# New due times for the steps woven into the expert rows, and the second half's weights held back until the last rows have landed

## The chip, the cores and the metric

The kernel runs on 1 core of one Trainium2 chip. The metric is the device time of one launch in microseconds (us), lower is better. A core has a matrix engine (PE, TensorE), a vector engine (DVE), a scalar engine (ACT), GpSimd (POOL) and a sync engine (SP) that here only issues transfers; each works through its own list of instructions in order and waits on semaphores. Transfers issued by SP and POOL run on the core's 16 DMA engines.

## The reference, cut to what matters

512 tokens of 1024 channels go through two blocks, all in 32-bit floats.

- First block: a convolution mixer, then a layer of experts. For each token 8 heads pick 16 of 16384 experts each, so 128 experts a token:

```python
u_sel = jnp.take(u, idx, axis=0)
act = jax.nn.gelu(jnp.einsum("chkd,cd->chk", u_sel, xc))
v_sel = jnp.take(v, idx, axis=0)
return jnp.einsum("chk,chkd->cd", act * gates, v_sel)
```

- Second block: a feed-forward layer (`x + 0.5 * (silu(x @ w_gate) * (x @ w_up)) @ w_down`, hidden width 2816), two causal attentions of 8 heads each (one with a forget gate, one with latent projections) whose outputs are gated, added and projected, and a second feed-forward layer of the same kind.

## The kernel before, in words

**Expert rows.** Tokens are held as 4 tiles of 128 (one token a partition). An expert "row" is one of the 512 pairs (tile, rank): for row `i`, POOL issues an indirect DMA (L2424) that gathers for each of the 128 tokens of tile `i // 128` its expert's `u` and `v` (128 x 2048 floats, 1 MB) into one of 7 buffers `pair`. DVE then forms the dot product (`dot`, L1728), ACT turns it into a weight with five tiny activations (`weigh`), and the weighted `v` is added to `resid`: for rows before 264 mostly by PE (a diagonal matmul), from row 264 on by DVE (`add_row`, L1062, 128 x 1024), two rows behind the dot. POOL may gather row `i` only when row `i - 7` was added.

**Two halves.** The second block is computed in two halves of 256 tokens. Half A (tiles 0 and 1, which are ready after 256 rows) runs while rows 264 to 511 are still being gathered; half B (tiles 2 and 3) runs after the last row. In half A, PE multiplies the weights as they come; in half B each weight chunk is first split into a rounded part and a rest (`rounded` on ACT, `split` on DVE), and three matmuls stand for one.

**Order of the woven steps.** PE runs half A's matmuls as fast as their inputs allow (it has no expert rows by then). On DVE, ACT and POOL, half A's steps are a generator that yields a due time before each step (`when(stage, n)`), and the class `Paced` releases, after expert row `i`, all steps that are due by `clock(i)`. So the place of each step among the rows is fixed when the program is built, by two things: the plan's clock (`Plan.add`, `Plan.ring` and the numbers in `plan_banks`, which add so many us for each use of a PSUM bank) and the table `PACE`, which says how many us each of the next so many rows is worth:

```python
def until(self, us):
    while self.due is not None and self.due <= us:
        self.due = next(self.steps, None)
```

I write "after row 499" for a step that stands after the dot of row 499 and the `add_row` of row 497. A step that is placed too early makes its engine wait, with all later rows behind it; one that is placed too late only makes PE's result sit in its bank.

**Stages of half A**: `norm1A`, `up1A` (22 chunks of gate and up weights, the products multiplied on DVE into `hidden`), `down1A` (4 banks: output half h, tile i; both tiles of one output half are finished almost together, since `rows_times` goes through the chunks with the two tiles inside), `norm_mA`, projections (`latA`, `fqA`, `fkA`, `fvA`), attention (38 steps n: the scores of head n are reduced on DVE at L1470 and exponentiated on ACT, transposed on PE three steps later, copied by ACT, multiplied with the values at step n + 4; after every 8 heads DVE scales the result into `ym`, L1056; PE also computes the gates of the output in between, `GATE_AT`), branches (`brA`), `woA`, and then the feed-forward stages `norm2A`, `up2A`, `down2A`.

**Weights.** SP issues the loads of all weight chunks (up to 1 MB each) in the order `ORDER` into three buffers `raw` (`loads`, `chunk`, L548); a load waits until the chunk three before it was used. For half A "used" is a PE semaphore; for half B it is the second part's split on DVE. The half's results are stored by SP as well (`store`, L566), where `ORDER` reaches chunk 3 of half B's first feed-forward layer.

Of the kernel before, what the change touches and what calls it, by code (L numbers as in the profile page):

```python
# [84 lines left out]
W = {}  # L85
# [6 lines left out]
NPAIR = 7  # L92
PAIRS = 512
# [1 line left out]
START_ROW = 264  # L95


PACE = ((64, 3.85), (25, 3.3), (28, 2.1), (36, 2.85), (22, 2.6), (64, 3.85), (PAIRS, 2.6))


def clock(row):

    at, left = 0.0, row - START_ROW
    if left < 0:
        return 2.6 * left
    for n, us in PACE:
        if left <= n:
# [27 lines left out]
class Plan:  # L135
# [4 lines left out]

    def add(self, stage, banks, us=0.0, told=True):

        n = sum(1 for k in self.uses if k[0] == stage)
        for j, b in enumerate(banks):
            self.fills[b] += told
            self.outs[b] += 1
            self.clock += us
            self.uses[stage, n + j] = Use(b, self.outs[b] - 1, self.fills[b], self.outs[b], self.clock)

    def ring(self, stage, n, us=0.0):  # L150
# [18 lines left out]
def plan_banks():  # L169
    p = Plan()  # L170
    for stage, n in (("norm0", 10), ("cf", 16), ("sc", 16), ("bg", 4)):
        p.ring(stage, n)
    p.add("y_sc", [0, 1, 4, 5])
    p.add("ms_sc", [6])
    p.add("y_sc", [2, 3, 7, 0])
    p.add("mean", [1])
    p.add("var", [1])
    p.add("ms_cf", [6, 7])
    p.add("y_cf", [4, 5, 2, 3, 6, 7, 4, 5])
    p.add("hn", [0, 1])  # L180
    for c, (h, a, b) in enumerate(CALLS):
        p.add("q", [0, 1])
        p.add("S", [2, 3])
        if c == 0:
            p.add("hn", [0, 1, 2, 3, 0, 1])
    for t in range(3):
        p.add("mix", [6, 7] if t == 1 else [4, 5], told=False)
    p.clock = 0.0
    for x in "AB":
        p.at = 6  # L190

        def ffn(f):
            p.clock += 8.0
            p.ring(f"norm{f}{x}", 4, 1.5)
            if x == "A":
                p.ring(f"up{f}{x}", 22, 7.0)
            else:
                for stage, n in (("up", 1), ("rate", 1), ("up", 21)):
                    p.ring(f"{stage}{f}{x}", n, 7.0)
            p.ring(f"down{f}{x}", 4, 19.0)  # L200

        ffn(1)
        p.clock += 8.0
        for stage, n, us in (("norm_m", 4, 1.5), ("lat", 2, 5.0), ("fq", 2, 7.0), ("ratem", x == "B", 0.0), ("fk", 2, 7.0),
                             ("cum", 1, 3.0), ("fv", 2, 7.0), ("tfq", 4, 1.0), ("tfk", 4, 2.0), ("tlat", 2, 1.0)):
            p.ring(stage + x, n, us)
        p.add("gate" + x, [4] if x == "A" else [5, 5], 6.0)
        p.add("look" + x, [0, 1] * 8, 3.3)
        p.add("look" + x, [0, 1] * 8, 6.2)
        p.add("turn" + x, [2, 3] * 16)  # L210
        p.add("prep" + x, [6, 7] * 8)
        for blk in range(4):
            p.add("o" + x, [4 + blk % 2], told=False)
            p.add("fin" + x, [4 + blk % 2], 2.0)
            if blk in (1, 2):
                p.add("gate" + x, [3 + blk])
        p.add("gate" + x, [6, 7, 6, 7, 6] if x == "A" else [6, 7, 6, 7])
        p.at = 0
        for stage, n, us in (("br", 16, 1.8), ("wo", 4, 7.0)):
            p.ring(stage + x, n, us)  # L220
        ffn(2)
    return p

# [63 lines left out]
def program(nc, x, meta, wts, uv, rows, cols, pos, ident, tri, mask, out):  # L287
    with ExitStack() as ctx:
# [3 lines left out]
        def sem(name):  # L292
            return ctx.enter_context(nc.semaphore(name))

        B = plan_banks().uses
# [58 lines left out]
        pairs_in = [sem(f"pair_landed{i}") for i in range(NPAIR)]  # L354
# [145 lines left out]
        def through(e, key):  # L500

            end = ENDS[key]
            if isinstance(end, int):
                e.wait_ge(w_used, end)
            else:
                e.wait_ge(full[B[end].bank], B[end].nth)
# [7 lines left out]
        def taken(e, stage, n):  # L514

            b = B[stage, n]
            e.wait_ge(outs[b.bank], b.after)
# [17 lines left out]
        def when(stage, n):  # L535
            return B[stage, n].when


        def loads(e):
            def chunk(c):  # L540
                if c.i >= 3:
                    was = W[ORDER[c.i - 3][0]]
                    if was.s is not None:
                        e.wait_ge(w_lo, 2 * was.s + 2)
                    else:
                        through(e, was.key)
                at_ = CHUNKS[c.key[0]][0] + c.key[1]
                e.dma_start(wbufs[c.slot][:, 0:c.n], wts[at_, :, 0:c.n]).then_inc(w_in[c.slot], 16)  # L548

            e.dma_start(h0[0:16, :], meta).then_inc(meta_in, 16)  # L550
            e.dma_start(resid[:, 0, :], x[0:P, :]).then_inc(x_in[0], 16)
            e.dma_start(idt[:], ident[0]).then_inc(const_in, 16)
            e.dma_start(colt[:], cols).then_inc(const_in, 16)
            for t in range(1, NT):
                e.dma_start(resid[:, t, :], x[t * P:(t + 1) * P, :]).then_inc(x_in[t], 16)
            for key, _ in ORDER[0:3]:
                chunk(W[key])
            for dst, src in ((onest, ident[1]), (ones1, ident[2]), (trit, tri), (maskf, mask), (rowt, rows),
                             (postt, pos)):
                e.dma_start(dst[:], src).then_inc(late_in, 16)  # L560
            def store(p):
                for h in range(2):
                    for i in range(2):
                        t = T0[p] + i
                        taken(e, "down2" + p, 2 * h + i)
                        e.dma_start(out[t * P:(t + 1) * P, h * 512:(h + 1) * 512],  # L566
                                    resid[:, t, h * 512:(h + 1) * 512]).then_inc(stored, 16)

            for key, _ in ORDER[3:]:
                if key == ("f1", 3, "B"):  # L570
                    store("A")
                chunk(W[key])
                if key == ("wout", 3):
                    filled(e, "bg", 3)
                    e.dma_start(kbuf, wts[CHUNKS["keys"][0]]).then_inc(keys_in, 16)
            store("B")
            e.wait_ge(stored, 16 * 2 * NT)
# [470 lines left out]
        def vector(e):  # L1048
# [414 lines left out]
            def attention(p):  # L1463
                t0, nth = T0[p], NTH[p]
                for n in range(38):
                    yield when("look" + p, min(n, 31))
                    if n < 32:
                        t, h, a = t0 + n % 16 // 8, n % 8, n // 8 % 2
                        o, _ = filled(e, "look" + p, n)
# [1 line left out]
                    if p == "B" and 3 <= n < 35:  # L1471
                        r = n - 3
# [13 lines left out]
                    if p == "B" and n >= 6 and (n - 6) % 8 == 7:  # L1486
                        r = (n - 6) // 8
# [4 lines left out]
                    if 4 <= n < 36 and (n - 4) % 8 == 7:  # L1492
                        r = n - 4
                        blk, a = r // 8, r // 8 % 2
# [314 lines left out]
        def scalar(e):  # L1809
# [257 lines left out]
            def attention(p):  # L2067
                t0, nth = T0[p], NTH[p]
                for n in range(38):
                    yield when("look" + p, min(n, 31))  # L2070
                    if n < 32:
                        h, a = n % 8, n // 8 % 2
                        w = (t0 + n % 16 // 8 + 1) * P
# [8 lines left out]
                    if p == "A" and 3 <= n < 35:  # L2082
                        r = n - 3
# [15 lines left out]
                    if n >= 6 and (n - 6) % 8 == 7:  # L2099
                        blk = (n - 6) // 8  # L2100
# [211 lines left out]
            for n in range(32):  # L2312
                steps = scores_in_steps(n + 2) if n < 8 else iter(())
                for k in range(16):
                    i, j = 16 * n + k, (16 * n + k) % 8
# [249 lines left out]
```

## Time and profile before

| | |
|---|---|
| median of 3 runs | 2482.41 us (2480.25 to 2482.93) |
| the profiled execution's own time | 2480.95 us |
| its span (first to last instruction) | 2479.1 us, 28622 instructions |
| mean granted TensorE clock | 0.932 |
| busy over the span | PE 85%, DVE 74%, ACT 48%, POOL 31% |
| moved by DMA | 760.89 MB: 536.90 MB by POOL's gathers, 222.15 MB by SP |

How to read it: the span falls into the first block's convolution (to about 250 us), the rows before 264 (to about 930 us), half A beside rows 264 to 511 (to about 1859 us) and half B (the rest). Busy shares are averages over these and don't tell what bounds any of them; for that the chain that ended last, the waits and the windows of one stage have to be read. In the timeline a group's row gives its start, its duration, and in brackets how long the engine sat idle before it and what released it. In a table of windows the columns are the busy time of PE, PE's weight load, DVE, ACT and POOL, then the granted clock, the DMA engines' busy share and GB/s.

### The profile page before, as it was taken

Reading aid. Unit: us, or ns where it says so; the run is one execution under the profiler, and the core shown is the slowest. Engines: PE = TensorE matmul, PEld = TensorE weight load, DVE = VectorE, ACT = ScalarE, POOL = GpSimd, SP = SyncE. Lnnn points to the kernel's source line nnn. Section 1 sums busy time; section 2 is a strip of 40 time slices with the busy share of each in tenths; the row PEclk is TensorE's granted clock in tenths of the full one; section 3 lists DMA queues with packets and bytes.
Section 4 is the critical chain, followed back from the end, with each engine's and each line's share of the span. In section 5 each row is a group of like instructions: output and inputs, shape, how many; then the busy total and the mean of one; then the engine's idle time right before and its main releaser. Section 6 shows DMA issues by size and latency. Waiting matters only on the chain.

```text
span 2479.1 us, 28622 instructions
## 1 busy us (share of the span) xinstructions
PE 2111.2 (85%) x9508; PEld 1500.0 (61%) x9508; DVE 1833.3 (74%) x3372; ACT 1180.2 (48%) x3776; POOL 760.6 (31%) x634
## 2 busy tenths in 40 slices
PE   6987898988877777999684578699949999999999
PEld 6965443443222225884343466488529988798997
DVE  6985676868888888887898987776576656567564
ACT  5214556555666664442455554433234436344443
POOL 0001444454555553232465643433220001100000
PEclk9988999999999998999795699899979999999999
DMA  5211999999999998999999999999984544124553
GB/s 210 72 68 58 382 415 421 417 413 421 421 421 420 415 417 346 387 419 398 379 417 353 363 414 365 396 397 421 386 355 170 187 167 167 69 86 155 186 187 136
DMA packets 107460, 760.89 MB, mean 307 GB/s; under 512 B 12064, under 2 KB 12832, under 8 KB 16432
## 3 DMA queue, kind: packets, MB, share of 16 engines
q0 software_dynamic: 73728, 536.90, 53.2%
q1 hardware_dynamic: 33584, 222.15, 23.7%
q8 instruction: 76, 1.25, 0.2%
q14 instruction: 72, 0.59, 0.1%
HBM read 756.91 MB, written 2.10 MB: 306 GB/s over the span
## 4 chain that ended last, share of the span: by engine, by line
PE 44%; DVE 9%; DMA 4%; issue 3%; ACT 1%; POOL 1%; DVEq 0%; ACTq 0%; POOLq 0%
PE bank L582 43%; DVE resid L1062 4%; DMA pair<-in_uv,idx 4%; DVE pair L1728 2%; PE bank L1019 0%; DVE half L1056 0%; DVE tmp L1056 0%; POOL smalls L2373 0%; PE bank L892 0%; POOL pair L2424 0%; DVE smalls L1384 0%; PE bank L825 0%; ACT half L1813 0%; DVE smalls L1470 0%; ACT frow L1813 0%
## 5 line engine op out<-in xcount | busy, mean ns | idle before, releaser
L2424 POOL DMA_INDIRECT pair<-in_uv,idx x512 | 649.6, 1269 | 874.8 <-DVE resid L1062 556.5
L1813 ACT ACTIVATE smalls<-smalls 128x1 f32<-128x1 f32 x2058 | 540.5, 286 | 665.1 <-DVE smalls L1728 647.0
L1728 DVE CUSTOM_DVE_ANT_0 pair<-pair,hn 128x1024 f32<-128x1024 f32 x512 | 624.1, 1220 | 155.4 <-DMA pair<-in_uv,idx 153.8
L582 PE MATMUL bank<-pair,diag 128*128 128x512 f32 x928 | 460.8, 629 | 118.2 <-ACT diag L1813 117.3
L582 PEld LDWEIGHTS bank<-pair,diag 128*128 128x128 f32 x928 | 169.3, 195 | 390.9 <-ACT diag L1813 245.9
L582 PE MATMUL bank<-ft,raw 128*128 128x256 f32 x1664 | 371.8, 387 | 12.0 <-DVE ft L1056 12.0
L1062 DVE SCALAR_TENSOR_TENSOR resid<-pair,smalls,resid 128x1024 f32<-128x1024 f32 x280 | 358.7, 1281 | 0.9 <-DVE resid L1062 0.5
L582 PEld LDWEIGHTS bank<-ft,raw 128*128 128x128 f32 x1664 | 323.1, 195 | 56.6 <-issue 12.5
L1056 DVE TENSOR_TENSOR half<-raw,half 128x1024 fp32r<-128x1024 f32 (+1 forms) x204 | 235.6, 1194 | 124.4 <-ACT half L1813 124.3
L1813 ACT ACTIVATE half<-raw 128x1024 fp32r<-128x1024 f32 (+1 forms) x204 | 199.4, 1025 | 129.0 <-PE bank L582 128.9
L582 PE MATMUL bank<-ft_hi,half 128*128 128x256 f32 x960 | 178.0, 286 | 2.6 <-DVE ft_early L1056 1.5
L582 PEld LDWEIGHTS bank<-ft_hi,half 128*128 128x128 f32 x960 | 150.9, 191 | 3.2 <-issue 1.8
L582 PE MATMUL bank<-raw,hidden 128*128 128x512 f32 x352 | 151.4, 593 | 0.0
L1813 ACT ACTIVATE smalls<-smalls,gat 128x1 f32<-128x1 f32 x512 | 143.2, 280 | 0.0
L582 PE MATMUL bank<-ft_late_hi,half 128*128 128x256 f32 x704 | 126.1, 282 | 2.3 <-DVE ft_late_lo L1056 2.3
L582 PE MATMUL bank<-ht,raw 128*128 128x512 f32 (+2 forms) x320 | 123.3, 529 | 0.7 <-ACT ht L1813 0.7
L2348 POOL TENSOR_TENSOR smalls<-smalls,mh 128x1 f32<-128x1 f32 (+1 forms) x21 | 15.8, 759 | 342.3 <-DVE smalls L1059 341.9
L582 PEld LDWEIGHTS bank<-raw,hidden 128*128 128x128 f32 x352 | 67.1, 191 | 83.1 <-issue 83.0
L582 PE MATMUL bank<-half,hidden_hi 128*128 128x512 f32 x352 | 110.9, 396 | 1.6 <-DVE half L1056 1.6
L582 PEld LDWEIGHTS bank<-ft_late_hi,half 128*128 128x128 f32 x704 | 108.4, 189 | 2.6 <-issue 2.5
L1813 ACT ACTIVATE diag<-idt,smalls 128x128 f32<-128x128 f32 x232 | 93.2, 402 | 21.4 <-ACT smalls L1813 0.4
L582 PE MATMUL bank<-ft_early,half 128*128 128x256 f32 x352 | 100.4, 285 | 0.0
(285 smaller groups left out, 2949.8 us busy)
## 6 DMA issues: line engine op xcount, KB each, us to landing
raw<-in_wts SPq DMA_DIRECT2D x196, 1024.0 KB, 6.0
pair<-in_uv,idx POOLq DMA_INDIRECT x512, 11.1
raw<-in_wts SPq DMA_DIRECT2D x10, 512.0 KB, 6.1
raw<-in_wts SPq DMA_DIRECT2D x4, 720.0 KB, 6.3
resid<-in_x SPq DMA_DIRECT2D x4, 512.0 KB, 6.2
out<-resid SPq DMA_DIRECT2D x8, 256.0 KB, 7.5
raw<-in_wts SPq DMA_DIRECT2D x2, 768.0 KB, 6.4
rowt<-in_rows SPq DMA_DIRECT2D x1, 1076.0 KB, 12.1
```

Of the source, the lines that this page charges most:

```text
L582: return e.matmul(o, a, b, start=start, stop=stop)
L1056: return e.tensor_tensor(o, a, b, op)
L1062: return e.scalar_tensor_tensor(out=o, in0=a, scalar=s, in1=b, op0=op0, op1=op1)
L1728: e.tensor_tensor_reduce(b[:, 0:1024], b[:, 0:1024], HN[i // 128], 1.0, 0.0, ALU.mult, ALU.add, actv[:, i % 8:i % 8 + 1]).then_inc(dotted, 1)
L1813: return e.activation(o, i, f, **kw)
L2348: e.tensor_tensor(nrs[0:n, c:c + 1], nqs[0:n, c:c + 1], mh[0:n, 0:1], ALU.pow).then_inc(n_rs, 1)
L2424: e.indirect_dma_start(pair[i % NPAIR], None, uv, bass.IndirectOffsetOnAxis(ap=idx[:, n % SLOTS, k:k + 1], axis=0)).then_inc(pairs_in[i % ...
```

## The change

Five edits. (1) `Plan.add` accepts a list of us, one for each bank use of a stage. (2) With it the first of the 22 `up` uses counts 12 us instead of 7, the four `down` uses 36, 2, 36, 2 instead of 19 each, the pairs of the projections and of `wo` three quarters and one quarter of their sum instead of halves, and `fin` 4 us instead of 2. (3) Attention's steps 32 to 37 are due 2.5 us apart instead of all with step 31 (`when_block`). (4) Two entries of `PACE` follow: 3.9 instead of 3.85 us a row for the 64 rows of each feed-forward layer, 3.05 instead of 2.85 for 36 rows of attention. (5) SP waits, before it loads chunk 1 of half B, until row 509 has landed, and half A's stores stand three chunks later, before chunk 6.

```diff
-PACE = ((64, 3.85), (25, 3.3), (28, 2.1), (36, 2.85), (22, 2.6), (64, 3.85), (PAIRS, 2.6))
+PACE = ((64, 3.9), (25, 3.3), (28, 2.1), (36, 3.05), (22, 2.6), (64, 3.9), (PAIRS, 2.6))
...
+        each = us if isinstance(us, tuple) else (us,) * len(banks)
         n = sum(1 for k in self.uses if k[0] == stage)
         for j, b in enumerate(banks):
             self.fills[b] += told
             self.outs[b] += 1
-            self.clock += us
+            self.clock += each[j]
...
             if x == "A":
-                p.ring(f"up{f}{x}", 22, 7.0)
+                p.ring(f"up{f}{x}", 22, (12.0,) + (7.0,) * 21)
...
-            p.ring(f"down{f}{x}", 4, 19.0)
+            p.ring(f"down{f}{x}", 4, (36.0, 2.0, 36.0, 2.0))
...
-        for stage, n, us in (("norm_m", 4, 1.5), ("lat", 2, 5.0), ("fq", 2, 7.0), ("ratem", x == "B", 0.0), ("fk", 2, 7.0),
-                             ("cum", 1, 3.0), ("fv", 2, 7.0), ("tfq", 4, 1.0), ("tfk", 4, 2.0), ("tlat", 2, 1.0)):
+        for stage, n, us in (("norm_m", 4, 1.5), ("lat", 2, (7.5, 2.5)), ("fq", 2, (10.5, 3.5)), ("ratem", x == "B", 0.0),
+                             ("fk", 2, (10.5, 3.5)),
+                             ("cum", 1, 3.0), ("fv", 2, (10.5, 3.5)), ("tfq", 4, 1.0), ("tfk", 4, 2.0), ("tlat", 2, 1.0)):
...
-            p.add("fin" + x, [4 + blk % 2], 2.0)
+            p.add("fin" + x, [4 + blk % 2], 4.0)
...
-        for stage, n, us in (("br", 16, 1.8), ("wo", 4, 7.0)):
+        for stage, n, us in (("br", 16, 1.8), ("wo", 4, (10.5, 3.5, 10.5, 3.5))):
...
+        def when_block(p, n):
+
+            return when("look" + p, min(n, 31)) + 2.5 * max(n - 31, 0)
...
             for key, _ in ORDER[3:]:
-                if key == ("f1", 3, "B"):
+                if key == ("f1", 1, "B"):
+                    r = PAIRS - 3
+                    e.wait_ge(pairs_in[r % NPAIR], 16 * (r // NPAIR + 1))
+                chunk(W[key])
+                if key == ("f1", 6, "B"):
                     store("A")
-                chunk(W[key])
...
-                    yield when("look" + p, min(n, 31))
+                    yield when_block(p, n)
```

The last pair of lines stands in the attention of DVE and, the same, in that of ACT.

What it moves. **DVE, end of half A's second feed-forward layer** (`pair_107` to `pair_113` are the 7 buffers, so a dot on `pair_113` is row 503 and one on `pair_107` row 504; `resid<-bank` is the add of a down result). Before, the fourth add stands after row 503 (the third, not shown, after row 499):

```order
2251 L1728 ISA pair_112,smalls<-pair_112,hn_83 128x1024
2252 L1728 ISA smalls 128x1
2253 L1062 SCALAR_TENSOR_TENSOR resid<-pair_110,smalls,resid 128x1024
2254 L1728 ISA pair_113,smalls<-pair_113,hn_83 128x1024
2255 L1728 ISA smalls 128x1
2256 L1062 SCALAR_TENSOR_TENSOR resid<-pair_111,smalls,resid 128x1024
2257 L1062 SCALAR_TENSOR_TENSOR resid<-bank,resid 128x512
2258 L1056 TENSOR_TENSOR colt<-colt 128x8
2259 L1728 ISA pair_107,smalls<-pair_107,hn_83 128x1024
```

In the changed kernel, where every line number below the edits is 10 higher, the third add stands after row 504 and the fourth after row 505:

```order
2253 L1738 ISA pair_113,smalls<-pair_113,hn_83 128x1024
2254 L1738 ISA smalls 128x1
2255 L1072 SCALAR_TENSOR_TENSOR resid<-pair_111,smalls,resid 128x1024
2256 L1738 ISA pair_107,smalls<-pair_107,hn_83 128x1024
2257 L1738 ISA smalls 128x1
2258 L1072 SCALAR_TENSOR_TENSOR resid<-pair_112,smalls,resid 128x1024
2259 L1072 SCALAR_TENSOR_TENSOR resid<-bank,resid 128x512
2260 L1738 ISA pair_108,smalls<-pair_108,hn_83 128x1024
```

So the first add of each output half moves five rows later (489 to 494, 499 to 504), the second one or two (494 to 495, 503 to 505); in the first feed-forward layer 313 to 318, 318 to 319, 323 to 328, and the last stays after row 328.

**DVE, end of attention.** Before, the last head's reduction and the last `ym` stand in the same place, after row 416:

```order
1941 L1728 ISA pair_110,smalls<-pair_110,hn_83 128x1024
1942 L1728 ISA smalls 128x1
1943 L1062 SCALAR_TENSOR_TENSOR resid<-pair_108,smalls,resid 128x1024
1944 L1470 TENSOR_REDUCE smalls<-bank 128x1
1945 L1496 RECIPROCAL smalls<-smalls 128x8
1946 L1056 TENSOR_TENSOR ym_138<-bank,smalls 128x512
```

In the changed kernel three rows stand between them (the reduction after row 414, `ym` after row 417):

```order
1938 L1480 TENSOR_REDUCE smalls<-bank 128x1
1939 L1738 ISA pair_109,smalls<-pair_109,hn_83 128x1024
1940 L1738 ISA smalls 128x1
1941 L1072 SCALAR_TENSOR_TENSOR resid<-pair_107,smalls,resid 128x1024
1942 L1738 ISA pair_110,smalls<-pair_110,hn_83 128x1024
1943 L1738 ISA smalls 128x1
1944 L1072 SCALAR_TENSOR_TENSOR resid<-pair_108,smalls,resid 128x1024
1945 L1738 ISA pair_111,smalls<-pair_111,hn_83 128x1024
1946 L1738 ISA smalls 128x1
1947 L1072 SCALAR_TENSOR_TENSOR resid<-pair_109,smalls,resid 128x1024
1948 L1506 RECIPROCAL smalls<-smalls 128x8
1949 L1066 TENSOR_TENSOR ym_138<-bank,smalls 128x512
```

ACT's copies for the last heads, all after row 416 before, now stand after rows 414, 415, 416 and 416. Nearly all other steps of half A on DVE and ACT stand one or two rows later than before or where they were (`hidden` in the second feed-forward layer one or two rows later); the last quarter of the heads stands one or two rows earlier. PE's list is the same. Nothing moves in half B but SP's stores.

## Rows read from the trace of the kernel before

**Rows 1.** The page: shares of the chain of work that ended last, by line

```profile
PE bank L582 43%; DVE resid L1062 4%; DMA pair<-in_uv,idx 4%; DVE pair L1728 2%; PE bank L1019 0%; DVE half L1056 0%; DVE tmp L1056 0%; POOL smalls L2373 0%; PE bank L892 0%; POOL pair L2424 0%; DVE smalls L1384 0%; PE bank L825 0%; ACT half L1813 0%; DVE smalls L1470 0%; ACT frow L1813 0%
```

**Rows 2.** Windows: all of half A, two stages, half B

```profile
929.00:1859.00 930.00, 737.06 (x2778) 525.06 (x2777) 735.98 (x1217) 402.42 (x1564) 376.31 (x300) 0.88 0.96 387
1400.00:1490.00 90.00, 58.94 (x273) 48.84 (x274) 79.02 (x112) 52.52 (x211) 47.24 (x36) 0.78 1.01 416
1640.00:1780.00 140.00, 140.00 (x577) 109.64 (x576) 85.61 (x116) 44.97 (x186) 42.52 (x38) 1.00 1.01 421
1859.00:2479.00 620.00, 605.72 (x4175) 557.04 (x4173) 367.47 (x561) 281.29 (x455) 24.73 (x19) 0.99 0.43 151
```

**Rows 3.** The chain in order of time, half A: start, length, what

```profile
962.10 228.35 PE bank L582 x876
...
1593.78 228.24 PE bank L582 x876
```

**Rows 4.** DVE's waits, 940 to 1240 us: total, times, longest

```profile
DVE resid L1062 <- PE bank L582: 12.0, 2, 10.9
DVE pair L1728 <- DMA pair<-in_uv,idx: 6.3, 9, 1.3
```

**Rows 5.** DVE's timeline, first feed-forward layer: add after row 313, add after row 328

```profile
1152.70 0.69 DVE L1062 SCALAR_TENSOR_TENSOR resid<-bank,resid 128x512 f32<-128x512 f32 x1 [10.93 <-PE bank L582]
...
1205.19 0.69 DVE L1062 SCALAR_TENSOR_TENSOR resid<-bank,resid 128x512 f32<-128x512 f32 x1
```

**Rows 6.** Windows behind the long waits: 1150, 1490, 1590 and 1780 us

```profile
1150.00:1180.00 30.00, 30.00 (x72) 13.30 (x71) 26.89 (x52) 9.67 (x43) 10.53 (x9) 1.00 0.95 374
1490.00:1520.00 30.00, 28.98 (x138) 25.25 (x137) 14.89 (x21) 13.63 (x36) 6.16 (x5) 0.96 0.82 312
1590.00:1630.00 40.00, 36.22 (x158) 31.60 (x159) 26.17 (x36) 14.29 (x55) 15.01 (x13) 0.91 0.89 343
1780.00:1800.00 20.00, 20.00 (x48) 8.81 (x47) 15.72 (x21) 6.88 (x30) 9.33 (x8) 1.00 0.83 306
```

**Rows 7.** DVE's timeline, attention: wait for fq, last head's reduction, last ym

```profile
1242.25 0.69 DVE L1056 TENSOR_TENSOR tmp<-fq 128x512 f32<-128x512 f32 x1 [2.35 <-ACT fq L1813]
...
1487.38 0.42 DVE L1470 TENSOR_REDUCE smalls<-bank 128x1 f32<-128x256 f32 x1
...
1499.88 0.69 DVE L1056 TENSOR_TENSOR ym<-bank,smalls 128x512 f32<-128x512 f32 x1 [11.24 <-PE bank L582]
```

**Rows 8.** DVE's waits, 1600 to 1850 us

```profile
DVE hidden L1056 <- ACT fsg L1813: 52.1, 22, 5.6
DVE resid L1062 <- PE bank L582: 26.7, 2, 17.0
```

**Rows 9.** DVE's timeline, the tail: dot 499, third down add, dot 505, last add of a row

```profile
1809.88 1.23 DVE L1728 CUSTOM_DVE_ANT_0 pair<-pair,hn 128x1024 f32<-128x1024 f32 x1 [1.30 <-DMA pair<-in_uv,idx]
...
1822.04 0.69 DVE L1062 SCALAR_TENSOR_TENSOR resid<-bank,resid 128x512 f32<-128x512 f32 x1 [9.73 <-PE bank L582]
...
1835.03 1.22 DVE L1728 CUSTOM_DVE_ANT_0 pair<-pair,hn 128x1024 f32<-128x1024 f32 x1
...
1857.04 1.28 DVE L1062 SCALAR_TENSOR_TENSOR resid<-pair,smalls,resid 128x1024 f32<-128x1024 f32 x1 [0.46 <-DVE resid L1062]
```

**Rows 10.** SP's timeline, 1815 to 1830 us

```profile
1820.32 3.76 SPq L548 DMA_DIRECT2D raw<-in_wts  x2
1824.12 1.64 SPq L566 DMA_DIRECT2D out<-resid  x3
```

**Rows 11.** ACT's timeline: half B's chunk 1 and chunk 2 rounded

```profile
1861.65 1.99 ACT L1813 ACTIVATE half<-raw 128x1024 fp32r<-128x1024 f32 x2
...
1872.16 1.99 ACT L1813 ACTIVATE half<-raw 128x1024 fp32r<-128x1024 f32 x2
```

**Rows 12.** Issue to landing, min, median, max: gathers from 1825 to 1841 us

```profile
DMA to landing us min/median/max: 8.8/10.6/10.9
```

**Rows 13.** The same: weight loads issued from 1819 to 1824 us

```profile
DMA to landing us min/median/max: 7.9/8.1/8.2
```

More of the change, by code:

```diff
@@ L2069, in attention @@
                 for n in range(38):
-                    yield when("look" + p, min(n, 31))
+                    yield when_block(p, n)
                     if n < 32:
```

## The prediction

> **What bounds the kernel now.** I read the page's chain first: PE's matmuls hold 43% of it, then DVE's row adds, the gathers and the dots [rows 1]. That is an average over stages, so I next read windows. Half A, 929 to 1859 us, has no engine full (PE 737, DVE 736 of 930 us), but the DMA engines are busy 0.96 of it at 387 GB/s; in the stretch where nothing stalls them they give 421 [rows 2]. Half B, 620 us, is PE at 605.7 busy [rows 2]; the change doesn't touch its matmuls, so all of the answer lies in half A and the seam.
>
> Then the chain in order of time. Two pieces are PE alone: 962.10 for 228.35 us and 1593.78 for 228.24 us, the two feed-forward layers [rows 3]. During them DVE's idle time costs nothing by itself; between and behind them the chain runs over DVE and the gathers. So half A's length is: the start of the first layer, 228 us, what DVE and DMA need to row 444 (where the second layer's input is complete), 228 us, and the tail of rows behind PE's end. Only the second stage and the tail can shrink.
>
> Last I looked for waits that hold rows up. DVE waits for PE's down results 12.0 us in the first layer (10.93 of it after row 313) [rows 4, 5] and 26.7 in the second [rows 8], and 11.24 us for the last `ym` of attention [rows 7]. While DVE waits, no buffer comes free, and just behind each wait the DMA rate drops: 374, 312, 343 and 306 GB/s instead of 421 [rows 6]. Those are the places where half A loses time that it can't make up, since DMA is near full elsewhere.
>
> **The change, part by part.** All against the profiled execution, 2480.95 us; the median shown is 1.5 us above it. No instruction is added on DVE, ACT, POOL or PE; SP gets one wait.
>
> *First layer's adds (rows 313 to 318 and 323 to 328).* PE finishes at 962.10 + 228.35 = 1190.5, yet the last add is reached at 1205.19 without a wait [rows 3, 5]: DVE is 14.7 us late there, 10.93 of it waited away earlier. Moving the adds takes the 12.0 us of wait out. How much arrives earlier depends on gathers: before the long wait DVE was already waiting for landings (9 waits, 6.3 us) [rows 4]. Lower end 3.3 us: the DMA time lost at 1150 to 1180, 30 x (421 - 374) / 421 [rows 6]. Upper end 12.0. I take **5**, nearer to the DMA end, because 12 us earlier means more gathers than 421 GB/s bring.
>
> *Projections.* The `fq` step on DVE moves two rows, more than its neighbours; its wait of 2.35 us [rows 7] is covered by a row. Ends 0 and 2.4, I take **2**. The wait for `lat` moves with its source and stays. Nothing is late next, since PE has whole banks in hand.
>
> *End of attention.* Before, the reduction of the last head is at 1487.38 and `ym` is ready 12.5 us later, at 1499.88 [rows 7]: all of steps 31 to 37 sit after row 416, and PE must still do two gate halves, transposes and products. Now three rows, about 7 us of DVE work (a row costs 2.34: five rows and two bank adds from 1822.04 to 1835.03 [rows 9]), stand in between. The wait falls to some 4 us, so DVE wins 7. But here DMA was at 416 GB/s just before [rows 2], so only lost DMA time counts: 30 x (421 - 312) / 421 = 7.8 us [rows 6], of which 7 / 11.24. Ends 0 and 7.8, I take **4.5**. The wait for the sigmoids behind it moves one row on both engines and stays.
>
> *The steps that are one or two rows later everywhere else.* Zero: each engine does the same work, and PE works ahead into 8 banks; its 228 us don't wait for `hidden` until the last chunk. The last step of the second layer's input stays after row 444, so that layer starts at the same row. POOL's rate for that norm moves one gather later with the mean that it waits for. Cover gone, this would cost one row, 2.3 us, at each norm.
>
> *The tail.* Before: DVE reaches the third down add after dot 499 (1809.88), waits 9.73 us, resumes at 1822.04, reaches dot 505 at 1835.03 and ends its rows at 1857.04 + 1.28 = 1858.3 [rows 9]. Now the third and fourth add stand after rows 504 and 505. If DVE is there when PE ends, rows 500 to 504 are already done: 1835.03 - 1822.04 = 13.0 us, less 1.3 for the two adds, 11.7 us won. For this the rows must have landed. From 1809.88, five rows of 1.05 MB at 421 GB/s are 12.5 us, to 1822.4, and one load of 1 MB more is 2.5; the DMA time that the waits lost (20 x 115 / 421 = 5.5 us at 1780 and 7.4 at 1590 [rows 6]) pays for that. Lower end: DVE at row 504 only at 1830, then 1830 + 1.3 + 23.3 = 1854.6, a gain of 3.7.
>
> *The held-back loads.* At 1820.32 and just after SP issues chunks 1 and 2 of half B, then the stores [rows 10]: 3 x 1.05 MB = 7.5 us at 421 GB/s, all between the last gathers. Before they cost little, as the tail was DVE's. With the down waits gone they would be what the last rows wait for; moved, the last landing (about 1850) can be 7.5 us earlier, which allows rows to end near 1848. The two edits need each other: together I take **10.5**, ends 3.7 and 11.7. The Trainium skill (DMA: Bandwidth & Descriptors, the table that opens the page) gives about 358 GB/s as one core's share of HBM; by that the same bytes would be 8.8 us. The trace moves 421 for 140 us on end [rows 2], so it isn't the limit here.
>
> *Chunks 1 and 2 arrive later.* Row 509 lands at least 9 us before the rows end; a load among gathers takes 7.9 to 8.2 us [rows 13]. So chunk 1 lands about when the rows end, chunk 2 two to three us later. ACT rounds them 3.4 and 13.9 us after that end (1861.65, 1872.16) [rows 9, 11]. Zero. The stores, now behind chunk 5, run where DMA is busy 0.43 [rows 2]: zero.
>
> Sum: 5 + 2 + 4.5 + 10.5 = 22 us. 2480.95 - 22 = 2459, with the 1.5 us to the median **2460**.
>
> **The rivals.**
>
> *DMA gives it back.* The bytes of half A are fixed, and where the waits go, waits for landings come. For: DMA at 0.96, DVE already waits for pairs. Against: four dips in [rows 6] are exactly behind the waits. Then only part of the lost DMA time returns upstream (3) and the tail wins 5: 2482.4 - 8 = 2474.
>
> *The change doesn't do what it says at the tail.* DVE reaches row 504 late, PE's end is no longer met, and upstream gains turn into idle time before the two 228 us pieces. Gain 0 to 3: 2481. Against: the second piece starts right behind DVE's last `ft` step, so earlier rows start it earlier.
>
> *Prefetch missed.* Two buffers stay empty at the seam. The Trainium skill (Trainium Kernel Development and Optimization, Best Practices) asks for transfers to overlap with compute by double buffering; this change gives some of that up. As a mechanism here: if a load takes as long as the slowest gather there (10.9 us [rows 12]) and row 509 lands only 5 us before the end, chunk 1 comes at +5.9 instead of +3.4 and ACT, with the rates of the last norm behind it, is 2.5 us late; chunk 2 the same: 5 us lost, 2465. By that rule the change would be worse than a kernel with the new due times alone; rows 10 to 13 speak against it.
>
> *Slower: attention's later heads.* Heads 19 to 31 stood on rows 390 to 416, and stand on 390 to 414. In the stretch 1400 to 1490 PE is busy 58.9 us for some 11 heads [rows 2], 5.4 each, and two rows with their reduction are 5.1. If each head's round trip (reduce, exponential, transpose, copy, product) becomes what DVE waits for, 12 heads at 2.3 us cost 28 us, 6 more than the 22 won: 2488. It decides once a round trip is longer than two rows. Against: PE's granted clock averages 0.78 in that stretch, part of the time 1.2 GHz and the rest 2.4, so it has speed left, and gathers at 2.5 us a row plus half a gate chunk allow 6.2 us a head.
>
> **How the numbers follow.** Forecast 0.55; DMA gives it back 0.20; prefetch missed 0.05; nothing gained 0.10; slower 0.10. All low ends (3 + 0 + 0 + 4) give 2475, all high ends (12 + 2.4 + 7.8 + 11.7 = 34) 2448.5. The range 2450 to 2476 takes in the second and third case. What can be told from no change is 0.2%, 5 us: faster means below 2477.4. Faster 0.79, same 0.12, slower 0.09.
>
> **What would show it.** Right: DVE's waits for PE's down results fall from 12.0 and 26.7 us to under 3 and 6; the last `ym` waits about 4; the second PE piece of 228 us starts some 11 us earlier (near 1582) and rows end near 1836; DVE has a little more wait for pairs; half B stays at 620 us. Wrong: the PE piece starts where it did; waits for pairs grow by what the down waits lost; a wait of ACT for chunk 1 or 2 at the seam; `look` waits in attention.

## The result, and the profile after

The changed kernel takes 2454.32 us (median of 6 runs, 2450.57 to 2458.89), the kernel before 2482.67 (6 runs, 2477.7 to 2486.1): ratio 0.9889, 95% interval [0.9871, 0.9906], 28 us faster (28.4 by the medians, 27.5 by the ratio). The profiled execution is one of the slowest of the six, 2458.72 us, with a span of 2456.9 us and a mean granted clock of 0.935.

Its own difference to the profile of before is 22.2 us. The timeline of DVE shows why it isn't 28: the dots of rows 264 (half A begins), 444 (the second feed-forward layer begins) and 511 (the last). Before:

```profile
943.70 1.22 DVE L1728 CUSTOM_DVE_ANT_0 pair<-pair,hn 128x1024 f32<-128x1024 f32 x1
...
1590.39 1.22 DVE L1728 CUSTOM_DVE_ANT_0 pair<-pair,hn 128x1024 f32<-128x1024 f32 x1
...
1852.77 1.22 DVE L1728 CUSTOM_DVE_ANT_0 pair<-pair,hn 128x1024 f32<-128x1024 f32 x1
```

After:

```profile
951.73 1.22 DVE L1738 CUSTOM_DVE_ANT_0 pair<-pair,hn 128x1024 f32<-128x1024 f32 x1
...
1582.26 1.22 DVE L1738 CUSTOM_DVE_ANT_0 pair<-pair,hn 128x1024 f32<-128x1024 f32 x1
...
1834.18 1.22 DVE L1738 CUSTOM_DVE_ANT_0 pair<-pair,hn 128x1024 f32<-128x1024 f32 x1
```

Row 264 comes 8.0 us later, and no instruction before it was changed; in the profiles of the experiments below it comes between 0.8 us earlier and 7.4 later than before. So I count from there. Rows 264 to 511 take 909.1 us before and 882.5 after, **26.6 us less**: 16.2 by row 444, 10.5 between rows 444 and 511. Half B, from the last row's add to the end, takes 620.8 and 617.2.

DVE's waits after, 940 to 1240 us (total, times, longest), against [rows 4]. The wait for PE's down results is gone, and waits for pairs have doubled from 6.3 us:

```profile
DVE hidden L1066 <- ACT fsg L1823: 17.5, 13, 3.6
DVE pair L1738 <- DMA pair<-in_uv,idx: 12.1, 13, 1.9
DVE smalls L1066 <- ACT lat L1823: 6.9, 1, 6.9
```

The same, 1480 to 1600 us. The last `ym` waits 3.5 us instead of 11.24 [rows 7] ("issue" stands where the view finds nothing that released it):

```profile
DVE pair L1738 <- DMA pair<-in_uv,idx: 9.0, 7, 2.2
DVE sigA L1066 <- ACT sigA L1823: 5.2, 1, 5.2
...
DVE ym L1066 <- issue: 3.5, 1, 3.5
```

The same, 1600 to 1850 us, against [rows 8]. The wait for PE falls from 26.7 to 10.8 us:

```profile
DVE hidden L1066 <- ACT fsg L1823: 47.0, 21, 4.1
DVE pair L1738 <- DMA pair<-in_uv,idx: 15.9, 12, 2.2
DVE resid L1072 <- PE bank L592: 10.8, 2, 5.5
```

Windows after, the first three where the DMA rate dropped before [rows 6], then the seam (columns as in [rows 6]):

```profile
1150.00:1180.00 30.00, 29.94 (x70) 13.04 (x70) 27.17 (x55) 8.97 (x42) 10.60 (x10) 1.00 1.01 421
1490.00:1520.00 30.00, 28.98 (x142) 25.31 (x141) 20.74 (x31) 15.11 (x47) 8.13 (x7) 0.99 1.01 411
...
1780.00:1800.00 20.00, 19.66 (x47) 8.54 (x46) 15.96 (x20) 7.91 (x35) 7.12 (x6) 1.00 1.01 421
...
1820.00:1830.00 10.00, 0.00 (x0) 0.00 (x0) 10.00 (x17) 4.36 (x21) 3.77 (x3) 0.57 0.98 374
1830.00:1840.00 10.00, 0.21 (x1) 0.21 (x2) 9.44 (x12) 6.15 (x18) 0.00 (x0) 0.50 0.26 109
```

374, 312 and 306 GB/s have become 421, 411 and 421. The whole stretch from dot 264 to dot 511, before and then after:

```profile
943.70:1852.77 909.07, 726.85 (x2755) 521.03 (x2753) 716.74 (x1180) 390.08 (x1519) 370.23 (x295) 0.88 0.97 389
951.73:1834.18 882.45, 734.43 (x2755) 523.41 (x2753) 717.43 (x1181) 389.45 (x1519) 357.38 (x295) 0.88 0.99 399
```

DVE does the same work (717 us), and the bytes are nearly the same: 909.07 us at 389 GB/s are 353.6 MB, 882.45 at 399 are 352.1. An estimate from these: at 399 GB/s the bytes of before take 886 us, so 23 of the 26.6 us are the higher rate, and the rest is 1.5 MB less in the stretch, about half A's stores (1.05 MB) that now stand behind it. The gain is DMA time that no longer stands idle. Where no wait for PE was moved, the rate still is low (343 GB/s before):

```profile
1300.00:1400.00 100.00, 53.78 (x191) 36.67 (x191) 85.93 (x139) 51.97 (x215) 52.10 (x38) 0.61 0.92 347
```

The chain in order of time, second feed-forward layer, against [rows 3]:

```profile
1586.84 189.43 PE bank L592 x784
1776.29 10.57 DMA raw<-in_wts
1786.90 29.46 PE bank L592 x68
```

This layer is still one stretch of PE, 229.5 us in all; the 1.2 us more than before stand beside the load of a weight chunk. The first layer is no longer on the chain as a piece: dots, adds, and four gathers of 15 to 16 us (1103.63, 1131.78, 1162.67, 1196.19) stand there instead. The page's chain by engine shows the same shift, before and then after; PE's one large line in it goes from 43% [rows 1] to 33%:

```profile
PE 44%; DVE 9%; DMA 4%; issue 3%; ACT 1%; POOL 1%; DVEq 0%; ACTq 0%; POOLq 0%
```

```profile
PE 34%; DVE 14%; DMA 6%; issue 4%; ACT 2%; POOL 1%; DVEq 0%; ACTq 0%; POOLq 0%
```

The tail on DVE after, dot 504, the third down add, and the last add of a row, against [rows 9]:

```profile
1808.66 1.23 DVE L1738 CUSTOM_DVE_ANT_0 pair<-pair,hn 128x1024 f32<-128x1024 f32 x1 [1.33 <-DMA pair<-in_uv,idx]
...
1816.39 0.69 DVE L1072 SCALAR_TENSOR_TENSOR resid<-bank,resid 128x512 f32<-128x512 f32 x1 [5.30 <-PE bank L592]
...
1838.45 1.28 DVE L1072 SCALAR_TENSOR_TENSOR resid<-pair,smalls,resid 128x1024 f32<-128x1024 f32 x1 [0.46 <-DVE resid L1072]
```

DVE is past row 504, which stood behind PE's end before, 5.3 us before PE ends. SP's two held-back loads and ACT's rounding of chunk 1, against [rows 10, 11]:

```profile
1823.57 1.18 SPq L555 DMA_DIRECT2D raw<-in_wts  x2
```

```profile
1843.06 1.99 ACT L1823 ACTIVATE half<-raw 128x1024 fp32r<-128x1024 f32 x2
```

Chunk 1 is rounded 3.3 us after the rows end (1839.7), as before, and without a wait. From 1833 to 1838 us the DMA engines move nothing (0 GB/s), so both loads have landed some 7 us before the rows end, earlier than the prediction had it.

### The profile page after: what moved, and what is told of

Read it like the earlier page. It is cut to its first block, busy times and chain, and to the rows that moved or that the text cites. A ratio compares the mean times of both kernels' runs of the same rounds, so it can differ in the third digit from the quotient of the medians.

```text
span 2456.9 us, 28623 instructions
## 1 busy us (share of the span) xinstructions
PE 2118.1 (86%) x9508; PEld 1502.4 (61%) x9508; DVE 1833.8 (75%) x3372; ACT 1179.7 (48%) x3776; POOL 742.2 (30%) x634
## 4 chain that ended last, share of the span: by engine, by line
PE 34%; DVE 14%; DMA 6%; issue 4%; ACT 2%; POOL 1%; DVEq 0%; ACTq 0%; POOLq 0%
PE bank L592 33%; DVE resid L1072 6%; DMA pair<-in_uv,idx 6%; DVE pair L1738 4%; ACT smalls L1823 0%; DVE tmp L1066 0%; DVE half L1066 0%; DMA raw<-in_wts 0%; PE bank L1029 0%; POOL smalls L2383 0%; DVE ohb L1066 0%; POOL pair L2434 0%; ACT L1823 0%; DVE smalls L1394 0%; PE bank L902 0%
## 5 line engine op out<-in xcount | busy, mean ns | idle before, releaser
L2434 POOL DMA_INDIRECT pair<-in_uv,idx x512 | 632.5, 1235 | 877.1 <-DVE resid L1072 531.5
L1823 ACT ACTIVATE smalls<-smalls 128x1 f32<-128x1 f32 (+1 forms) x2058 | 540.1, 286 | 642.8 <-DVE smalls L1738 622.8
L592 PE MATMUL bank<-pair,diag 128*128 128x512 f32 x928 | 455.8, 623 | 125.2 <-ACT diag L1823 124.8
L592 PE MATMUL bank<-ht,raw 128*128 128x512 f32 (+2 forms) x320 | 128.8, 547 | 0.7 <-ACT ht L1823 0.7
L2358 POOL TENSOR_TENSOR smalls<-smalls,mh 128x1 f32<-128x1 f32 (+1 forms) x21 | 15.9, 761 | 339.6 <-DVE smalls L1069 339.3
L592 PEld LDWEIGHTS bank<-ht,raw 128*128 128x128 f32 x320 | 63.4, 219 | 64.3 <-issue 58.4
```

Of the source, the lines that this page charges most:

```text
L592: return e.matmul(o, a, b, start=start, stop=stop)
L1823: return e.activation(o, i, f, **kw)
L2358: e.tensor_tensor(nrs[0:n, c:c + 1], nqs[0:n, c:c + 1], mh[0:n, 0:1], ALU.pow).then_inc(n_rs, 1)
L2434: e.indirect_dma_start(pair[i % NPAIR], None, uv, bass.IndirectOffsetOnAxis(ap=idx[:, n % SLOTS, k:k + 1], axis=0)).then_inc(pairs_in[i % ...
```

## The experiments

The theory was the prediction's: DVE waits cost DMA time, the due times take them away, and the held-back loads are needed for the tail's part. The rivals were that the loads carry nothing, or that the terms cover each other. "Rows" below is the time from dot 264 to dot 511 in the run's profile, less the 909.1 us of before. A ratio goes by runs of the kernel before that were made beside it; their medians are 2481.31 (due_only to mid_only), 2481.04 (layer1_only to late_nohold) and 2480.19 (the last four).

| kernel | median us | ratio to before | rows us |
|---|---|---|---|
| changed kernel | 2454.32 | 0.9889 [0.9871, 0.9906] | -26.6 |
| due_only | 2456.14 | 0.9893 [0.9877, 0.9908] | -24.8 |
| hold_only | 2482.92 | 1.0004 [0.9993, 1.0016] | -1.7 |
| ffn_only | 2459.77 | 0.9921 [0.9905, 0.9938] | -20.2 |
| mid_only | 2473.79 | 0.997 [0.9958, 0.9982] | -7.9 |
| layer1_only | 2478.9 | 0.999 [0.9978, 1.0002] | -5.0 |
| layer2_only | 2472.24 | 0.9963 [0.995, 0.9976] | -8.4 |
| late | 2456.27 | 0.9893 [0.9876, 0.991] | -29.1 |
| late_nohold | 2456.04 | 0.99 [0.9882, 0.9917] | -23.4 |
| block_only | 2477.88 | 0.999 [0.998, 1.0] | -5.9 |
| after_no_block | 2454.38 | 0.9894 [0.988, 0.9908] | -22.3 |
| waits | 2453.16 | 0.9898 [0.9883, 0.9913] | -29.5 |
| waits_late | 2446.61 | 0.9875 [0.9859, 0.9891] | -33.0 |

An interval is 2.5 to 4.3 us to each side. The rows have scatter too: layer2_only and hold_only give every engine the same order up to row 444, and reach it, counted from row 264, 3.0 us apart.

**The two edits apart.** due_only is the changed kernel with SP's loop as before:

```diff
-                if key == ("f1", 1, "B"):
-                    r = PAIRS - 3
-                    e.wait_ge(pairs_in[r % NPAIR], 16 * (r // NPAIR + 1))
-                chunk(W[key])
-                if key == ("f1", 6, "B"):
+                if key == ("f1", 3, "B"):
                     store("A")
+                chunk(W[key])
```

> The new due times alone; SP's loads and stores stand as before the change. Theory of the prediction (the edits need each other): the three transfers, 3.15 MB or 7.5 us at 421 GB/s, sit between the last gathers and take about that from the tail's gain, so the gain over the kernel before is about 21 us instead of 28 (ratio 0.9915), and DVE waits for pairs behind PE's end. Rival (the hold is worth nothing): in the changed kernel the DMA engines are nearly idle from 1830 us on while the rows end at 1840, and dot 511 waits for nothing, so the gain stays within 2 us of 28 (ratio 0.989).

hold_only is the kernel before with the lines marked - above in place of those marked +.

> SP's hold and the moved stores alone, on the kernel before. Both theories: the tail of the kernel before is DVE's own (1.0 us of waits for pairs), so gain 0 to 1.5 us, ratio 0.9994 to 1.0. Rival (moved bytes pay by themselves): 5 to 7.5 us, ratio 0.997.

The due times alone give 25.2 us by the medians and 26.5 by the ratio, against 28.4 and 27.5 of the changed kernel; the 0.9915 of the theory lies outside the interval. The loads alone give nothing that can be told. So the edits don't need each other: the rival came true. Windows of due_only at the seam:

```profile
1820.00:1830.00 10.00, 0.00 (x0) 0.00 (x0) 7.80 (x13) 3.75 (x16) 0.56 (x1) 0.50 0.98 401
1830.00:1840.00 10.00, 1.97 (x8) 1.57 (x8) 9.21 (x11) 5.57 (x14) 0.00 (x0) 0.50 0.05 20
```

With the loads among the gathers, DMA is still all but done at 1830, and dot 511 is at 1832.0, with adds until 1837.5. But the loads do delay the last rows a little. Dots 508, 509 and 510 wait for their gathers in due_only, 2.2 us together, and in the changed kernel no dot behind row 504 waits. Dot 508 in both:

```profile
1821.26 1.23 DVE L1735 CUSTOM_DVE_ANT_0 pair<-pair,hn 128x1024 f32<-128x1024 f32 x1 [1.08 <-DMA pair<-in_uv,idx]
```

```profile
1824.76 1.21 DVE L1738 CUSTOM_DVE_ANT_0 pair<-pair,hn 128x1024 f32<-128x1024 f32 x1
```

The reason that it isn't more lies in the landings that the two traces record. In the changed kernel rows 506 to 510 have landed 3.7 to 4.7 us before DVE reaches their dots, since DVE stood 5.3 us for PE just before. In due_only they have landed 2.8 us (row 506), 1.4 (507) and 0 (508 to 510) before. This slack took most of the loads' 7.5 us: rows 504 to 511 take 26.9 us there and 25.5 in the changed kernel, rows 444 to 511 253.8 and 251.9.

**The due times in two groups.** ffn_only and mid_only hold the loads back, and keep the new numbers of the feed-forward layers alone, or all the others alone (projections, `fin`, `when_block`, `wo` and the entry 3.05 of `PACE`). mid_only against the changed kernel; ffn_only takes back exactly what this leaves:

```diff
-PACE = ((64, 3.9), (25, 3.3), (28, 2.1), (36, 3.05), (22, 2.6), (64, 3.9), (PAIRS, 2.6))
+PACE = ((64, 3.85), (25, 3.3), (28, 2.1), (36, 3.05), (22, 2.6), (64, 3.85), (PAIRS, 2.6))
...
-                p.ring(f"up{f}{x}", 22, (12.0,) + (7.0,) * 21)
+                p.ring(f"up{f}{x}", 22, 7.0)
...
-            p.ring(f"down{f}{x}", 4, (36.0, 2.0, 36.0, 2.0))
+            p.ring(f"down{f}{x}", 4, 19.0)
```

> The hold and only the feed-forward layers' due times (up, down, 3.9 us a row); attention, projections and wo stand by the old numbers. By the rows of the two profiles, counted from row 264, the feed-forward layers won 11 us up to row 328 and 10.5 from row 444 to the end, attention 7 to 10 in between. Theory (the terms add up): gain about 19 us, ratio 0.992. Rival (DMA gives upstream gains back): what is not won in attention is not lost either, gain 26 or more; or the first layer's 11 us vanish in attention and only the tail's 10 to 12 stay, ratio 0.9955.

> The hold and only the due times between the two layers (projections, fin, when_block, wo, 3.05 us a row in attention). Theory: the last ym's wait falls from 11 to 4 us and the fq wait goes: gain 7 to 10 us, ratio 0.9965. Rival (bound by DMA there): 0 to 3 us.

By the ratios 19.6 and 7.4 us, by the rows 20.2 and 7.9: together as much as the whole (both runs hold the loads back, which is worth 1.7 us of rows by itself). Both theories came true. The two groups neither cover nor need each other, within intervals of 3 to 4 us each.

**The two layers apart.** layer1_only against ffn_only; layer2_only has `f == 2` and the other 3.85:

```diff
-PACE = ((64, 3.9), (25, 3.3), (28, 2.1), (36, 2.85), (22, 2.6), (64, 3.9), (PAIRS, 2.6))
+PACE = ((64, 3.9), (25, 3.3), (28, 2.1), (36, 2.85), (22, 2.6), (64, 3.85), (PAIRS, 2.6))
...
-                p.ring(f"up{f}{x}", 22, (12.0,) + (7.0,) * 21)
+                p.ring(f"up{f}{x}", 22, ((12.0,) + (7.0,) * 21) if f == 1 else 7.0)
...
-            p.ring(f"down{f}{x}", 4, (36.0, 2.0, 36.0, 2.0))
+            p.ring(f"down{f}{x}", 4, (36.0, 2.0, 36.0, 2.0) if f == 1 else 19.0)
```

> The hold and the first feed-forward layer's due times alone. In the profiles counted from row 264, row 328 comes 11 us earlier than before, row 444 (by the run with both layers) 8.5. Theory (rows won in the first layer are lost by half in attention, and the rest starts the second layer earlier): gain about 8 us, ratio 0.9967. Prediction's term: 5 us (0.998). Rival (the tail's PE-bound end swallows it): 0 to 2.

> The hold and the second layer's due times alone: the first add of each output half 4 to 5 rows later, the last one row later. Theory: PE's 228 us piece starts where it did, the five rows that stood behind its end are done before it: gain 10 to 12 us, ratio 0.9955. Rival (without the first layer's gain DVE is not at row 504 when PE ends): 4 to 6 us, ratio 0.998.

2.5 and 9.2 us, and 19.6 for both. For the first layer the theory's 8 us lie outside the interval (-0.5 to 5.5 us), and the prediction's 5 inside it; for the second, 9.2 (6.0 to 12.4) takes in the theory and leaves out its rival's 0.998. DVE's waits, 1600 to 1860 us, layer1_only, then layer2_only:

```profile
DVE resid L1072 <- PE bank L592: 29.4, 2, 19.9
```

```profile
DVE resid L1072 <- PE bank L592: 9.4, 3, 5.1
```

layer1_only reaches row 444 5.2 us earlier, but the add after row 489 stands where it did and waits 19.9 us. Rows 444 to 511 take 262.5 us in it, 252.3 in layer2_only and 250.7 in ffn_only; that part stands by itself. Before row 444 the rows gain 5.2, -1.7 and 8.5 us; a part of what is missing is scatter, and why the two give less apart than together is left open.

**Later adds in the tail.** late is the changed kernel with the adds of the second layer after rows 497, 497, 508 and 509, late enough that none waits for PE; late_nohold the same with SP's loop as before:

```diff
-            p.ring(f"down{f}{x}", 4, (36.0, 2.0, 36.0, 2.0))
+            p.ring(f"down{f}{x}", 4, (36.0, 2.0, 36.0, 2.0) if (f, x) != (2, "A") else (46.0, 2.0, 35.0, 2.0))
```

> The changed kernel with the second layer's down adds later still: after rows 497, 497, 508, 509 instead of 494, 495, 504, 505. Theory: in the changed kernel DVE still waits 5.3 us for PE after row 504; now four more rows stand before that, so the tail is the gathers' (2.5 us a row) and 3 to 5 us shorter than in the changed kernel: ratio 0.987. Rival: the last gathers are what DVE then waits for, gain 0 to 1 over the changed kernel.

> The same without the hold (SP's loads and stores as before the change). Theory: the hold is worth little only because PE's end bounds the tail; once it doesn't, 7.5 us of transfers stand before the last rows, so this one is 3 to 6 us slower than with the hold and no faster than the changed kernel. Rival: the hold stays worth 1.5 us or less.

DVE's waits for pairs, 1600 to 1860 us, late, then late_nohold; neither has a wait for PE's down results:

```profile
DVE pair L1738 <- DMA pair<-in_uv,idx: 23.7, 16, 2.5
```

```profile
DVE pair L1735 <- DMA pair<-in_uv,idx: 28.7, 19, 2.6
```

The 10.8 us of waiting for PE became 7.8 us more for gathers: behind PE the tail is bound by landings. The theory of 3 to 5 us less than the changed kernel missed: rows 444 to 511 take 249.9 us, 2.0 less. Here the held-back loads do show, 5.0 us of waits and 5.7 us of rows, 4.6 of them between rows 444 and 511 where the loads stand. But the times are equal, and equal to due_only's. Part of it lies in the profile of late itself, whose half B takes 623.2 us against 617.2 in late_nohold. A window of 165 us that starts 260 us behind the last row (attention of half B), late, then late_nohold:

```profile
2094.10:2259.10 165.00, 161.26 (x1158) 148.04 (x1157) 106.14 (x182) 71.72 (x141) 9.81 (x6) 0.97 0.30 109
```

```profile
2096.10:2261.10 165.00, 162.31 (x1189) 148.39 (x1187) 109.69 (x187) 75.39 (x146) 9.82 (x6) 1.00 0.30 109
```

The granted clock there is 0.97 in one and 1.00 in the other for the same work: for some 10 us it is at 1.2 GHz instead of 2.4, and 0.03 x 165 = 5 us of full speed are missing. In the same window of the 14 profiles this clock is 0.99 or 1.00 in nine, whose half B takes 617.2 to 618.7 us and once 619.8, and 0.97 or 0.98 in five, whose half B takes 620.4 to 623.2; the kernel before (620.8, 0.98) is one of these five, the changed kernel (617.2, 1.00) one of the nine. So the 2.5 us of rows between late and the changed kernel can't be told in a median of six runs.

**The end of attention.** block_only holds the loads back and has `when_block` alone; after_no_block is the changed kernel without it:

```diff
-                    yield when_block(p, n)
+                    yield when("look" + p, min(n, 31))
```

> The kernel before with the held-back loads and stores and, of the due times, only the end of attention (steps 32 to 37 of attention 2.5 us apart; the numbers of the other stages and both tables as before). My term for it was 4.5 us (0 to 7.8). Theory 'the last ym is what mid_only won by': 2475 to 2478, DVE's wait for the last ym falls from 11.2 to about 4, rows from 416 to 420 take some 8 us less. Rival 'the shift of fin, the projections and the pace won it': 2481 within 2 us, because three rows between the reduction and ym only move the wait to the sigmoids behind.

> The changed kernel without the end of attention: steps 32 to 37 are again all due with step 31, everything else as changed. Theory 'each term stands by itself': 4 to 8 us slower than the changed kernel, 2459 to 2462, with the wait of about 11 us for the last ym back. Rival 'the second layer and the tail take it up': rows between 420 and 444 catch up, since two rows of buffers are landed there, and it is within 2 us of 2454.

DVE's waits, 1410 to 1600 us, block_only, then after_no_block:

```profile
DVE ym L1066 <- issue: 3.1, 1, 3.1
```

```profile
DVE ym L1066 <- PE bank L592: 9.6, 1, 9.6
```

The wait falls by 8 us in the one and comes back in the other. From the rows it is worth some 4: 5.9 in block_only less the 1.7 of hold_only, and 4.3 between after_no_block and the changed kernel. The medians don't show it: block_only is 2.3 us under before, and after_no_block is as fast as the changed kernel (2454.38), which is what its rival said; within some 4 us on each side that neither confirms nor excludes 4.

**Two more waits.** waits moves, on the changed kernel, DVE's first use of `lat` and the first product with the sigmoids 5 us later; waits_late does the same on late:

```diff
-        for stage, n, us in (("br", 16, 1.8), ("wo", 4, (10.5, 3.5, 10.5, 3.5))):
+        for stage, n, us in (("br", 16, (6.8,) + (1.8,) * 15), ("wo", 4, (5.5, 3.5, 10.5, 3.5))):
...
-                yield when("lat" + p, 1)
+                yield when("lat" + p, 1) + 5.0
...
-                yield when("lat" + p, 1) + 4.0
+                yield when("lat" + p, 1) + 9.0
```

(the + 5.0 on DVE and before `forgets` on ACT).

> The changed kernel with two more steps moved: DVE's first use of lat and ACT's and DVE's steps on the forget gates behind it 5 us later (wait of 6.9 us in the changed kernel), and DVE's first product with the sigmoids 5 us later (wait of 5.2 us), the first wo step 5 us closer behind it. Theory 'waits of DVE cost the DMA time behind them, some 0.6 of their length, as those of the change did': 12 us of wait give 5 to 7 us, 2447 to 2450. Rival 'DMA has nothing to make up there, the rate is already 419 to 424 behind them': 2452 to 2456, waits for pairs grow by what the two lose.

> The same two moves on the kernel whose down adds of the second layer stand after rows 497, 497, 508, 509. Theory 'the tail is bound by landings once DVE doesn't wait for PE': as the kernel with the two moves alone, within 2 us of it. Rival 'with the rows earlier, the later adds pay': 3 us or more below it.

DVE's waits of waits_late, 1100 to 1600 us:

```profile
DVE smalls L1066 <- ACT lat L1823: 2.9, 1, 2.9
...
DVE sigA L1066 <- ACT sigA L1823: 0.3, 1, 0.3
```

The two waits were 6.9 and 5.2 us in the changed kernel; 8.9 us of them are gone, and row 444 comes 3.5 us earlier than there. waits itself is not to be told from the changed kernel: its 2453.16 is in its rival's range and not in the theory's 2447 to 2450, and 2.9 us of rows came of 8.6 us of waits (3.1 and 0.4 left). waits_late is 33.6 us under before, and 6.5 under waits: the rival, that the later adds pay once the rows come earlier, is what the rows (3.5 us between the two) and the medians say. It is the fastest kernel of the study; its interval overlaps the changed kernel's, so that it beats that one is likely and not shown.

## Why the prediction was right, and where it was not

The time (2460, range 2450 to 2476) and its mechanism held: the gain is DMA time lost behind DVE's waits. By its own steps:

- **First layer, 5 us.** After row 328 the changed kernel was 11.2 us ahead, near the upper end of 12; by row 416 it was 7.2, since DVE's waits for pairs between the two rows are 15.4 us and were 11.6. layer1_only keeps 5.0 of rows, 2.5 by the ratio. The choice "nearer to the DMA end" was right, though the give-back lay between rows 328 and 390, not inside the layer.
- **Projections, 2 us.** mid_only less block_only (projections, `fin`, `wo`, 3.05): 2.0 us of rows, 5 by the ratios. Within the scatter.
- **End of attention, 4.5 us.** Some 4 by the rows; not seen in the time of after_no_block.
- **Tail and held-back loads, 10.5 us.** 10.5 by the rows from 444 to 511. But the split was wrong, so that the term came out to the tenth is luck. The step that failed is "With the down waits gone they would be what the last rows wait for", and with it "The two edits need each other": I priced three transfers at 7.5 us and took DMA as the bound to the last row. due_only lost 1.8 us of rows (1.9 from 444 to 511), so nearly all of the 10.5 is due times. What I didn't count is the wait for PE that stays in the tail: while DVE stands 5.3 us behind row 504, the next rows land, 3.7 to 4.7 us before their dots. Only with that wait out of the way too (late) did the loads cost rows 5.7 us.
- **"The wait for PE under 6 us in the tail"**: it is 10.8, 5.5 at the first add and 5.3 at the third. The rows came earlier than the step allowed for, so DVE is ahead of PE at both. The second piece of PE starts 635.1 us after row 264 and before it was 650.1: 15.0 us earlier, where I had some 11. late took these waits and found gathers behind them.
- **The zeros** held: no wait for chunk 1 or 2 at the seam. The steps and the stores that moved showed no cost.
- **What was missing**: 22 was the sum, 26.6 the rows, 28.4 the medians. It lies between rows 416 and 444, which gave 9.0 us where a term of 4.5 stood; up to row 416 and behind row 444 the terms came out. block_only and after_no_block give the end of attention some 4 of the 9.0, and what the rest belongs to stays open. Half B's 3.6 us go with the granted clock of its attention (0.98 before, 1.00 after); none of its steps moved but SP's stores.

Of the rivals, "DMA gives it back" is what each profile shows in small (12.1 for 6.3 us, 15.9 for 10.4 of waits for pairs) without deciding. "Prefetch missed" did not occur: the two loads were issued late, and nothing waited. The Trainium skill (Trainium Kernel Development and Optimization, Best Practices) wants transfers to overlap with compute by double buffering. hold_only, which puts off two of its prefetches, is at 1.0004 [0.9993, 1.0016], so the rule shows neither gain nor loss here. "Attention's later heads" did not come either: rows 390 to 416 take 77.3 us after and 77.0 before.

## What to carry to other kernels

Where a program's order is fixed beforehand by due times, read each wait of the engine that frees the buffers together with the DMA rate just behind it: what a wait costs is nearer to the transfer time lost in the dip than to its own length. Here the four dips of before add up to 24 us (3.3 + 7.8 + 7.4 + 5.5) of the 26.6 won, but a single dip is a rough price (3.3 us against the 5.0 of rows that layer1_only keeps, 7.8 against some 4 for the end of attention). An edit that keeps transfers out of each other's way is worth little as long as the delayed transfers still land before the engine that consumes them gets there; look for that slack, above all behind a wait of that engine, before pricing the edit by its bytes. Split a change of many small moves into groups and compare the time between two fixed points of the program, since differences of 2 to 5 us are hidden in the run-to-run scatter of the parts that weren't touched.

## What the runs showed of the hardware that was not expected

- Stretches with unchanged instructions scatter more than I had allowed for: row 264 is reached between 942.9 and 951.7 us in 14 profiles (dot), half B takes 617.2 to 623.2 us with the granted clock of its attention between 1.00 and 0.97.
- The seam took two loads that were issued only when row 509 had landed at no cost (hold_only, 1.0004), and three transfers among the last gathers at 2 us of the 7.5 that their bytes need at 421 GB/s (due_only): the rows behind 505 had landed up to 4.7 us before DVE came to them.
- One core moves 420 or 421 GB/s from 1650 to 1750 us in the profiles of ffn_only, layer1_only, layer2_only and block_only alike, as before. The Trainium skill (DMA: Bandwidth & Descriptors, the table that opens the page) gives about 358 GB/s as a core's share of HBM; the traces don't agree. Its section on bandwidth says that one core alone was measured at 425 with transfers of 16 MB, and the traces agree with that to about 1%, with transfers of 1 MB in a queue.
